# A modulation head with products of 128 equal columns and fillers, and layer ends with banks weighed ahead of the norm

## What is computed

```
h = rms_norm(x, norm_mix[i]) * (1 + sc1) + sh1
y = attention with relative bias (layer 0) or spatial gating (layer 1)
x = x + g1 * y
h = rms_norm(x, norm_ffn[i]) * (1 + sc2) + sh2
x = x + g2 * (square(relu(h @ ffn_w1[i])) @ ffn_w2[i])
```

```
h = rms_norm(x, pre_norm_g[l])
ya, yb = differential attention, grouped attention (both gated)
y = concat(ya, yb) @ w_out[l]
x = x + rms_norm(y, post_norm_g[l])
```

## Time and profile before

| | |
|---|---|
| median of 3 runs | 1052.47 us (1052.29 to 1052.95) |
| the profiled execution | 1056.26 us, its span 1054.6 us |
| TensorE busy | 1021.9 us, 97% of the span |
| VectorE busy | 765.9 us, 73% |
| ScalarE busy | 550.3 us, 52% |
| GpSimd busy | 101.9 us, 10% |
| DMA | 218.46 MB, 207 GB/s over the span |

### The profile page before, as it was taken

One profiled execution on the slowest core, in us unless ns is written; L12 is line 12 of the kernel. 1 busy time (PEld: TensorE's weight loads), 2 busy tenths in 40 slices (PEclk: granted clock), 3 DMA queues, 4 the chain that ended last, 5 costly groups with the idle time before them and its releaser, 6 DMA issues.

```text
span 1054.6 us, 17080 instructions
## 1 busy us (share of the span) xinstructions
PE 1021.9 (97%) x6048; PEld 893.3 (85%) x6048; DVE 765.9 (73%) x1368; ACT 550.3 (52%) x918; POOL 101.9 (10%) x160
## 2 busy tenths in 40 slices
PE   6999998999999999999999999999999999899996
PEld 5888877899999988889999899999988888788885
DVE  5688878997888677787778756555568786587863
ACT  1457666644544466744444445444346676566662
POOL 0030201000000010010010000000003021030210
PEclk9999999999999999999999999999999999999999
DMA  9876665688787648857686455666526640175501
GB/s 368 298 264 217 226 215 201 225 311 298 265 282 271 227 149 314 293 200 260 210 278 201 145 190 168 194 210 198 164 96 234 204 156 21 65 265 182 167 12 41
DMA packets 57197, 218.46 MB, mean 207 GB/s; under 512 B 6420, under 2 KB 11540, under 8 KB 51000
## 3 DMA queue, kind: packets, MB, share of 16 engines
q1 hardware_dynamic: 48368, 169.24, 47.0%
q0 software_dynamic: 6048, 43.52, 11.5%
q10 hardware_dynamic: 2728, 5.00, 1.6%
HBM read 216.67 MB, written 1.06 MB: 206 GB/s over the span
## 4 chain that ended last, share of the span: by engine, by line
PE 86%; DVE 7%; DMA 3%; ACT 3%; issue 1%; POOL 0%; SPq 0%; ACTq 0%; DVEq 0%
PE ps L1746 25%; PE ps L1748 25%; PE ps L1747 25%; PE ps L1857 2%; PE ps L2229 2%; DVE w_lo L1008 2%; DMA ada_raw<-in_adastream 1%; PE ps L1805 1%; PE ps L2121 1%; PE ps L2277 1%; PE ps L1795 1%; DMA arena<-in_adastream 1%; ACT w_hi L554 1%; DMA raw<-in_wstream 1%; DVE h_lo L1087 1%
## 5 line engine op out<-in xcount | busy, mean ns | idle before, releaser
L1008 DVE TENSOR_TENSOR w_lo<-raw,w_hi 128x1024 fp32r<-128x1024 f32 (+1 forms) x312 | 356.3, 1182 | 62.6 <-ACT w_hi L554 57.8
L554 ACT ACTIVATE w_hi<-raw 128x1024 fp32r<-128x1024 f32 (+1 forms) x312 | 306.7, 1020 | 135.5 <-DMA raw<-in_wstream 97.5
L1746 PE MATMUL ps<-h_hi,w_hi 128*128 128x256 f32 x704 | 200.8, 285 | 0.7
L1748 PE MATMUL ps<-h_hi,w_lo 128*128 128x256 f32 x704 | 199.2, 283 | 0.0
L1747 PE MATMUL ps<-h_lo,w_hi 128*128 128x256 f32 x704 | 199.2, 283 | 0.0
L1746 PE MATMUL ps<-w_hi,h_hi 128*128 128x512 f32 (+1 forms) x480 | 190.6, 397 | 4.6 <-DVE h_lo L1087 2.9
L1748 PE MATMUL ps<-w_hi,h_lo 128*128 128x512 f32 (+1 forms) x480 | 184.9, 385 | 0.0
L1747 PE MATMUL ps<-w_lo,h_hi 128*128 128x512 f32 (+1 forms) x480 | 184.8, 385 | 0.0
L1746 PEld LDWEIGHTS ps<-h_hi,w_hi 128*128 128x128 f32 x704 | 134.9, 192 | 3.9 <-DVE h_lo L1087 1.6
L1746 PE MATMUL ps<-w_hi,a_hi 128*128 128x512 f32 x352 | 137.3, 390 | 0.6 <-DVE a_lo L1463 0.6
L1747 PE MATMUL ps<-w_lo,a_hi 128*128 128x512 f32 x352 | 137.2, 390 | 0.0
(11 more groups left out here) (221 smaller groups left out, 1316.9 us busy)
## 6 DMA issues: line engine op xcount, KB each, us to landing
raw<-in_wstream SPq DMA_DIRECT2D x296, 512.0 KB, 5.3
ada_raw<-in_adastream POOLq DMA_DIRECT2D x40, 1024.0 KB, 5.3
ada_raw<-in_adastream SPq DMA_DIRECT2D x4, 1024.0 KB, 9.2
arena<-in_adastream SPq DMA_DIRECT2D x4, 1024.0 KB, 10.7
row<-in_gate_rows ACTq DMA_DIRECT2D x5, 512.0 KB, 4.0
raw<-in_wsmall SPq DMA_DIRECT2D x16, 128.0 KB, 2.3
row<-in_params POOLq DMA_DIRECT2D x2, 769.0 KB, 5.2
x<-in_x SPq DMA_DIRECT2D x1, 1024.0 KB, 9.4
```

The lines of the kernel that those rows point to most:

```text
L554: act.activation(w_hi[:, c % SPLIT, at], raw[:, n, 0:width // 2], ACT.Copy)\
L1008: nc.vector.tensor_tensor(w_lo[:, c % SPLIT, at], raw[:, (2 * c + h) % RAW, 0:width // 2], w_hi[:, c % SPLIT, at].bitcast(F32), ALU.subtract)\
L1746: nc.tensor.matmul(dst, sh, mh, start=start, stop=False)
L1748: return nc.tensor.matmul(dst, sl, mh, start=False, stop=stop)
```

## The change

`FIRST_PE` becomes (1, 3, 5, 7), so that VectorE sums four chunks instead of five. Chunks 6 and 7 swap their places in memory, and the waits in `first` follow. A first product multiplies each tile by a column of `cond` repeated 128 times (64 where the bank ends), so that every result stands in 64 to 128 equal columns; results are 64 columns apart in banks 0 and 1 and are read with a stride of 64 (`first_modulation`). The sums go through `first_columns`, 64 columns wide, in turns with the products instead of all together at the end. `keep_warm_first(n)` issues n f32 products of the table `cols` with itself, 128 x 128, whose result nobody reads: 14 ahead of chunk 1, 3 ahead of the transposes, 5 ahead of chunk 7 and 11 behind the last columns, in the place of the eight of zeros. The second half of weight chunk 0 gets its low part behind the modulation instead of ahead of it. GpSimd's load of chunk 8 waits for chunk 5's product and one sum instead of four sums.

At the layer ends VectorE first multiplies a bank by the gain row (`weigh`, waiting for ScalarE's square of the bank alone), and later scales by the inverse root and adds `x` in one instruction (`post_residual`), in the order weigh 0, 1, residual 0, 1, weigh 2, 3, residual 2, 3. GpSimd takes the first bank's mean plus epsilon as soon as it has it and adds the second's. The result is stored in four pieces of 256 KB.

```diff
--- before.py
+++ after.py
@@ -49,7 +49,7 @@
 ADA_KEPT = 16
 ADA_AT = 14
 FIRST_ADA = 8
-FIRST_PE = (1, 3, 6)
+FIRST_PE = (1, 3, 5, 7)
 
 
 C_QKV = 0
@@ -235,7 +235,7 @@
 
         first_ada = [v.rearrange("p (k n) -> p k n", n=AW) for v in (
             spare[:, 0:CW], part(8192, CW), spare[:, CW:2 * CW], part(4096, CW), part(6144, CW),
-            spare[:, 0:CW], part(8192, CW), spare[:, CW:2 * CW])]
+            spare[:, 0:CW], spare[:, CW:2 * CW], part(8192, CW))]
         t5_row = probs[0:4, 1, :]
         zeros4 = zero_row[:].unsqueeze(1).to_broadcast([1, 4, P])
         dist = nc.dram_tensor("t5_by_distance", [4, 512], F32).ap()
@@ -360,9 +360,9 @@
                         .then_inc(s_raw[n % RAW], 16)
 
             def first(a):
-                if a in (5, 7):
-                    sp.wait_ge(s_ada, (a - 3) // 2)
-                if a == 6:
+                if a in (5, 6):
+                    sp.wait_ge(s_ada, a - 4)
+                if a == 7:
                     sp.wait_ge(s_first_used, 1)
                 sp.dma_start(first_ada[a].rearrange("p k n -> p (k n)"), adastream[a])\
                     .then_inc(s_first[a], 16)
@@ -401,10 +401,12 @@
                     load(C_SECOND + 4 + k, wstream[layer * 16 + C_SECOND + row_k], CW,
                          layer * (2 * C_LAYER))
 
-            for t in range(TT):
-                sp.wait_ge(s_xb, 4 * DEPTH + 2 * (t + 1))
-                sp.dma_start(out[t * P:(t + 1) * P, :], x[:, t, :]).then_inc(s_stored, 16)
-            sp.wait_ge(s_stored, 32)
+            for i in range(4):
+                t, cb = divmod(i, 2)
+                v = slice(cb * 512, (cb + 1) * 512)
+                sp.wait_ge(s_xb, 4 * DEPTH + (i + 1))
+                sp.dma_start(out[t * P:(t + 1) * P, v], x[:, t, v]).then_inc(s_stored, 16)
+            sp.wait_ge(s_stored, 64)
 
 
         @block.gpsimd
@@ -453,7 +455,8 @@
                     pool.wait_ge(s_qss, 2 * q + t + 1)
                     rinv(rinv8[:, t], mean8[:, t], ss8[:, t], DH, s_qr)
 
-            ada_load(adastream[8], 0, 4)
+            pool.wait_ge(s_first_used, 3)
+            ada_load(adastream[8], 0, 1)
             ada_load(adastream[9], 1, 8)
             head_rinv(0)
             ada(10, 1)
@@ -531,11 +534,16 @@
                     nc.gpsimd.tensor_tensor(rinv8[:, 0, v], mean8[:, 1, v], rpre[:],
                                             ALU.mult).then_inc(s_yq, 1)
                 for t in range(TT):
-                    pool.wait_ge(s_ysq, layer * 4 + 2 * (t + 1))
-                    own.inc(nc.gpsimd.tensor_tensor(ss2[:, t:t + 1], yss[:, t, 0:1],
-                                                    yss[:, t, 1:2], ALU.add))
+                    pool.wait_ge(s_ysq, layer * 4 + (2 * t + 1))
+                    own.inc(nc.gpsimd.tensor_scalar(ss2[:, t:t + 1], yss[:, t, 0:1], 1.0 / D, EPS,
+                                                    ALU.mult, ALU.add))
                     own.wait()
-                    rinv(rinv2[:, t:t + 1], mean2[:, t:t + 1], ss2[:, t:t + 1], D, s_yr)
+                    pool.wait_ge(s_ysq, layer * 4 + (2 * t + 2))
+                    own.inc(nc.gpsimd.tensor_scalar(mean2[:, t:t + 1], yss[:, t, 1:2], 1.0 / D,
+                                                    ss2[:, t:t + 1], ALU.mult, ALU.add))
+                    own.wait()
+                    nc.gpsimd.tensor_tensor(rinv2[:, t:t + 1], mean2[:, t:t + 1], half[:, 0:1],
+                                            ALU.pow).then_inc(s_yr, 1)
 
 
         @block.scalar
@@ -1160,17 +1168,29 @@
                 ada_sum(first_ada[a], ada_acc[:, (a + ADA_AT) % ADA_KEPT, :],
                         a - len([b for b in FIRST_PE if b < a]) or None)
 
+            def first_modulation():
+
+                dve.wait_ge(s_modps, 1)
+                nc.vector.tensor_tensor(mod_shift[:, 0], ps[:, 0, 0:512:64], cols[:, COL_ADA:COL_ADA + 8],
+                                        ALU.add)
+                own.inc(nc.vector.tensor_tensor(mod_scale[:, 0], ps[:, 1, 0:512:64],
+                                                cols[:, COL_ADA + 8:COL_ADA + 16], ALU.add))
+                own.wait()
+                nc.vector.scalar_tensor_tensor(mod_scale[:, 0], mod_scale[:, 0], 1.0,
+                                               cols[:, COL_NORM:COL_NORM + 8],
+                                               ALU.add, ALU.mult).then_inc(s_mod, 1)
+
             first_sum(0)
             norm_x(0)
             first_sum(2)
             dve.wait_ge(s_t5ps, 1)
-            nc.vector.tensor_copy(t5_row, ps[0:4, 1, :]).then_inc(s_t5c, 1)
+            nc.vector.tensor_copy(t5_row, ps[0:4, 2, :]).then_inc(s_t5c, 1)
             first_sum(4)
-            first_sum(5)
-            first_sum(7)
+            first_sum(6)
             dve.sem_inc(s_ada, len(FIRST_PE))
-            split(0)
-            modulation(0, 0)
+            lo_part(0, 0, CW)
+            first_modulation()
+            lo_part(0, 1, CW)
             operand(0)
             split(1)
             split(2)
@@ -1723,16 +1743,33 @@
                     lsplit(21, SMALL)
 
 
-                for i in range(4):
+                weighed = {}
+
+                def weigh(i):
+
                     t, cb = divmod(i, 2)
-                    if cb == 0:
-                        dve.wait_ge(s_yr, layer * 2 + (t + 1))
-                    own.inc(nc.vector.scalar_tensor_tensor(
-                        y_tmp[:, i, :], ps[:, cb * 2 + t, :], rinv2[:, t:t + 1],
-                        row[:, R_POST + cb * 512:R_POST + (cb + 1) * 512], ALU.mult, ALU.mult))
-                    own.wait()
+                    dve.wait_ge(s_ysq, layer * 4 + (i + 1))
+                    weighed[i] = own.inc(nc.vector.tensor_tensor(
+                        y_tmp[:, i, :], ps[:, cb * 2 + t, :],
+                        row[:, R_POST + cb * 512:R_POST + (cb + 1) * 512], ALU.mult))
+
+                def post_residual(i):
+
+                    t, cb = divmod(i, 2)
+                    dve.wait_ge(s_yr, layer * 2 + (t + 1))
+                    own.wait(weighed[i])
                     v = x[:, t, cb * 512:(cb + 1) * 512]
-                    nc.vector.tensor_tensor(v, v, y_tmp[:, i, :], ALU.add).then_inc(s_xb, 1)
+                    nc.vector.scalar_tensor_tensor(v, y_tmp[:, i, :], rinv2[:, t:t + 1], v,
+                                                   ALU.mult, ALU.add).then_inc(s_xb, 1)
+
+                weigh(0)
+                weigh(1)
+                post_residual(0)
+                post_residual(1)
+                weigh(2)
+                weigh(3)
+                post_residual(2)
+                post_residual(3)
                 if layer + 1 < DEPTH:
                     lsplit(22, SMALL)
 
@@ -1847,31 +1884,59 @@
                                      stop=True)
 
 
-            pe.wait_ge(s_cond, 1)
+            def first_column(a, b, width=64):
+
+                j = 2 * a + b
+                at = j % 8 * 64
+                return ps[:, j // 8, at:min(at + width, 512)]
 
             def first_product(a):
 
                 pe.wait_ge(s_first[a], 16)
                 for b in range(2):
+                    dst = first_column(a, b, P)
                     for k in range(KT):
                         last = nc.tensor.matmul(
-                            ps[:, 0, 2 * a + b:2 * a + b + 1],
-                            first_ada[a][:, k, b * P:(b + 1) * P], cond[:, k:k + 1],
+                            dst, first_ada[a][:, k, b * P:(b + 1) * P],
+                            cond[:, k:k + 1].to_broadcast([P, dst.shape[1]]),
                             start=k == 0, stop=k == KT - 1)
-                last.then_inc(s_first_used, 1)
-
-            first_product(FIRST_PE[0])
+                return last.then_inc(s_first_used, 1)
+
+            def first_columns(a, done):
+
+                pe.wait_ge(s_ada, done)
+                for b in range(2):
+                    dst = first_column(a, b)
+                    last = nc.tensor.matmul(
+                        dst, ada_acc[:, (a + ADA_AT) % ADA_KEPT, b * P:(b + 1) * P],
+                        ones[:, 0:dst.shape[1]], start=True, stop=True)
+                return last
+
+            def keep_warm_first(n):
+
+                for _ in range(n):
+                    nc.tensor.matmul(ps[:, 3, 0:P], cols[:, 0:P], cols[:, 0:P], start=True,
+                                     stop=True)
+
+            pe.wait_ge(s_cond, 1)
+            keep_warm_first(14)
+            first_product(1)
+            pe.wait_ge(s_set, 4)
+            first_columns(0, 1)
+            keep_warm_first(3)
             pe.wait_ge(s_in, 16)
             transpose_x(0)
             pe.wait_ge(s_relb, 32)
-            nc.tensor.matmul(ps[0:4, 1, :], probsT[0:32, 0, 0:4], probs[0:32, 0, :], start=True,
+            nc.tensor.matmul(ps[0:4, 2, :], probsT[0:32, 0, 0:4], probs[0:32, 0, :], start=True,
                              stop=True).then_inc(s_t5ps, 1)
```

(14 more changed lines are left out.)

## The result

The changed kernel takes 1046.97 us (median of 5 runs, 1046.73 to 1048.71), the kernel before, on the same chip, 1052.89 (5 runs, 1052.29 to 1053.92): ratio 0.9934, interval 0.9917 to 0.9952. It is 5.9 us faster, where 14.5 were forecast, and 1046.97 lies above the range (1035 to 1045). The profiled execution took 1046.97 us, its span is 1045.3.

What follows compares the result with a forecast made beforehand. Bound by TensorE's products (86% of the span), with the first 48 us at the lower clock level. 8.7 + 2.6 - 0.8 + 1.65 + 2.4 = 14.55 us; the unprofiled median 1052.47 minus 14.5 gives 1038.0, range 1035 to 1045.

Steps and rivals of the forecast that it cites:

- the baseline: Whole kernel: stretches of the profiled execution (1056.26) are the same in unprofiled runs, median 1052.47; minus 14.5 is 1038.0.
- the stall at head 0: At head 0, TensorE waits for VectorE's third low part: a cost of 0.8 us, bounds 0 and 2.2.
- the landings in the start: Ada chunks 4 to 7 land at 19.6, 22.1, 24.7 and 27.2 us, counted back from first weights at 28.5.
- the gain ahead of 48 us: Main products from 42.9 to 48.4 us take 0.23 us each instead of 0.43: 2.6 us gained.
- The start: First modulation: fillers and equal columns lift TensorE's clock by 9.1 us; first main product 34.15 instead of 42.88, 8.7 us.
- rival (a): Start, between 13.8 and 17.8 us: the clock level rises but falls again; 1039 to 1042 us, chance 0.29.
- the queue doesn't run dry: Start's loads: ada chunks 4 and 5 are still under way when chunk 6 goes at 19.4 us.
- VectorE's lag: Ahead of head 0: VectorE leaves the operand 8.0 us earlier, TensorE 11.3; VectorE regains some 1.4, running 9.4 earlier.
- The other stretch: Dip between 130 and 137 us, 3.4 us at half speed, costing 1.7; left in the sum, its absence in the range.
- The layer ends: Plain products ahead of the inverse root, halved stores: 1.65 us at the first layer, 2.4 at the last.
- Rival (b): Start: equal f32 columns don't lift the clock level at all; +5.2, 1057.7 us, chance 0.11.
- Rival (c): Head stage takes the start's gain back: nothing of the 2.6 and half of the 8.7 arrive; 1045 us, chance 0.05.

Runs made afterwards that it cites:

- the second trace: The kernel before, unchanged, run and traced once more: 1053.37 us, ratio 0.9998, span 1051.5.
- hold_ada: Changed kernel with ada chunk 8's load held behind all first sums and chunk 9's behind chunk 0's low parts: 1047.45 us, ratio 0.9921.
- no_fillers: Changed kernel without its 33 filler products in the start, the 128 equal columns kept: 1047.00 us, ratio 0.9919.
- late_loads: Changed kernel with the third weight chunk loaded ahead of bias, flip and rope loads, and ada chunk 9 held back: 1047.96 us, ratio 0.9929.
- start_only: Changed kernel with the layer ends of the kernel before, so the new start alone: 1051.62 us, ratio 0.9962 (0.9945 to 0.998).
- ends_only: Kernel before with only the new layer ends, its start kept: 1050.43 us, ratio 0.9956.
- first group: Experiments on one chip: before again, start alone, layer ends alone, fillers left out; the kernel before there has 28 runs, median 1053.85 us.

## Why the prediction was wrong

The forecast gain exceeded the real one by 8.6 us. The steps that failed, each told below, are the baseline (3.1), the stall at head 0 (1.4) with a drop of the clock behind it that the sum doesn't have (1.6), the landings in the start (1.6) and the gain ahead of 48 us (1.0). What is smaller nearly cancels.

**The baseline: failed.** "Those stretches are the same in unprofiled runs, whose median is 1052.47; minus 14.5 is 1038.0." They aren't. The sum was made on an execution of 1056.26, 3.8 above the median, with the start at the lower level up to 48.3 us; the second trace, whose time (1053.18) is near that median, has part of its start at the upper one (39.75 against 42.88). Of the 8.6 us by which the forecast gain exceeded the real one, 3.1 are this: 9.3 us of span against the trace before, 6.2 against the second one, and the medians differ by 5.9. The sign was there to be read: the forecast noted the two numbers and explained their distance by nothing. How much the step costs is the chip's share of each start: on the third chip, where most executions of before have the slow one, hold_ada gains 8.6 us and not 5.9. Even there 14.5 isn't reached.

**The start: right, 1.6 us short.** First main product 7.10 earlier, forecast 8.7. The level rises within the fillers and holds; none of the slow stretches of rival (a) falls in the start. That the fillers do it was needed for nothing: without them the first chunk product raises the level itself, and the total stays (no_fillers). The missing 1.6 are landings: chunk 5 at 23.5 (22.1 forecast), chunk 7's product at 28.79 (27.2), the table behind the 32-row product at 17.6, though "the queue doesn't run dry". Counting back from the first weights' landing assumed that it would stay; it moved from 28.5 to 29.8. Of this delay some 0.3 is GpSimd's earlier load (at 27.70 instead of 29.16, 1.5 us and not 4). In no_fillers chunk 7's landing ends a wait of TensorE at 28.27, 1.1 later than forecast, with no product in its way.

**The lower level ahead of 48 us: right in kind, 1.0 short.** 2.6 forecast. From the first product to the last ahead of head 0 the change gains another 1.56 (8.66 less 7.10); 0.70 of what is missing is a wait of TensorE at 47.66 for a low part of the late third chunk, a small form of the same lag.

**VectorE's lag: mis-sized; with the clock's drop behind it the step that cost most in the kernel itself (3.0 us).** The forecast let VectorE regain "some 1.4" of its lag, since "the 1.49 us that it idles before 51.36 are a wait for weights that will then be there". They were not there: an engine that comes 8 us earlier meets a load that doesn't, and it idles 4.00 us. The wait at head 0 is 2.14, with what stands beside it 2.5 against 0.3 before; so a cost of 2.2, the upper bound, for a forecast of 0.8.

**The clock drops behind the wait: not in the sum.** 1.6 us from 77.6 to 80.9, gone when fillers are put into the wait; what else it takes is open, since the wait of 2.27 us in late_loads had none of it. Rival (a) had such a price (1.7), but looked for it in the start. The other stretch, at 133 before, appears at 128.6 after, and cost the same: 1.7 by the clock of the earlier trace rows, 0.06 and 0.11 of two 10 us windows after. In the second trace of before it is absent (clock 1.00 from 120 to 140), so against that one the kernel after pays it anew. It begins 1 us behind a wait of TensorE of 0.67 us in both, which the second trace has too; what brings it no run shows.

**The layer ends: right.** First layer 1.53 (5.63 to 7.16; forecast 1.65), last 2.2 (2.4 forecast; 8.32 to 6.09 from the last main product's start to the span's end). The order of steps is the one that the prediction gives.

The sum against the trace before: 7.1 + 1.56 - 2.2 - 1.6 + 0.8 (small gains and losses up to 180 us, the other stretch among them) + 1.5 + 2.2 = 9.3, the roundings and a loss of 0.1 behind 920 us in it. Rival (b), that equal f32 columns don't lift the level, is wrong for 128 of them; with a single column in their place the level doesn't hold, and most of (b)'s picture comes about. Rival (c), the head stage takes it back, came nearer than its chance of 0.05 says: half of what it named happened, its argument against (TensorE busy 46.44 of 50 us) being from a stretch behind the one that decides.

## What to carry to other kernels

Before a forecast is taken from one profiled execution, hold its time against the runs: where it is some tenths of a per cent above their median, part of what the trace offers to remove isn't there in the others. When one engine is made early, follow each engine beside it to the load that it will meet, since loads stay where the queue and the bandwidth put them. And weigh a wait of TensorE in front of dense products at more than its length: of the five of 2 us or more that these traces have behind their first chunk, four were followed by 3.4 to 6.8 us at half speed. Moving one piece of VectorE work behind what TensorE waits for gave 4.3 us between two variants on one chip, where the whole new start had given 2 to 6 on another (the interval of start_only).

## What the hardware showed that was not expected

- The recorded clock counts full speed up to its first change. Of the 28 executions of the kernel before on the first group's chip, the slower 10 record 0.993 to 0.997 and take 1055.8 to 1058.1 us, the others 0.984 to 0.988 and 1052.3 to 1055.5. Over all chips the two sorts overlap a little in time: one run at 0.997 takes 1054.68.
- Whether transposes and a 32-row product lift the level differs from execution to execution of one program: at 19.9 us in one trace of the kernel before, not at all until 48.3 in the other, nor until 48.2 in ends_only, whose start is the same.
- The length of an idle time of TensorE alone doesn't tell whether the level falls. It fell in or behind 2.86 us (at 35 us, without fillers), 2.14 (at 77, after) and 2.27 (at 76.6, hold_ada), and not behind the 2.27 before 76.22 in late_loads, nor behind 1.26 and 0.73 in the start. The stretch near 130 us begins behind a wait of only 0.67 in the kernels before and after.
- Columns of an f32 product cost next to nothing up to 128: at the upper level the starts of 128-column pieces are 0.115 us apart (3.67 and 3.68 us for the 32 of chunks 1 and 5), those of 64-column pieces 0.098 and 0.113 (0.39 and 0.45 us for 4). The Trainium skill ("TensorE: Matmul & The Clock Gate", Back-to-back issue gap) has 60 and 134 cycles for these two, one about twice the other, as the gap of products by themselves, and says that in a stream with weight loads both set the pace; for f32, with a weight load to each piece, the trace has the two within 2 to 17% of each other.
